# Output projection's second half in another block order with its sums shared with GpSimd, and the down projection's first splits moved ahead of the up projection's end

## The reference, cut to what matters

```python
h = h + merged @ w_out                                  # output projection, here called M
hn = rms_norm(h, mlp_norm_g)
h = h + jnp.square(jax.nn.relu(hn @ w_up)) @ w_down     # up projection U, down projection D
return h[:, N_META:]
```

## Time and profile before

| what | value |
|---|---|
| median of 3 runs | 1728.98 us (1727.06 to 1730.18) |
| profiled execution, its own time | 1731.9 us |
| its span | 1730.2 us |
| PE busy in the span | 1672.7 us, 97% |
| DVE, ACT, POOL busy | 923.8, 745.9, 384.5 us |
| M's second half | about 1035.5 to 1085 us |
| U | 1092.08 to about 1414 us |
| D | 1419.65 us to the end |

### The profile page before, as it was taken

One profiled execution on the slowest core, in us unless ns is written; L12 is line 12 of the kernel. 1 busy time (PEld: TensorE's weight loads), 2 busy tenths in 40 slices (PEclk: granted clock), 3 DMA queues, 4 the chain that ended last, 5 costly groups with the idle time before them and its releaser, 6 DMA issues.

```text
span 1730.2 us, 22462 instructions
## 1 busy us (share of the span) xinstructions
PE 1672.7 (97%) x7968; PEld 1385.3 (80%) x7968; DVE 923.8 (53%) x1712; ACT 745.9 (43%) x1528; POOL 384.5 (22%) x587
## 2 busy tenths in 40 slices
PE   7999999999999999898999999699999989999999
PEld 6777888878878888786888888488888878888887
DVE  4311256522355666645654425866666645766776
ACT  5322245423356666655212215555555444444443
POOL 1000001010037777675211001112211222200000
PEclk9999999999999999999999999899999999999999
DMA  6111113211123443426545223145444359843463
GB/s 193 50 49 48 46 60 116 71 61 49 49 67 76 99 97 70 101 56 173 185 144 188 74 61 123 48 148 175 147 140 154 138 196 345 280 127 98 123 194 98
DMA packets 109061, 204.08 MB, mean 118 GB/s; under 512 B 12560, under 2 KB 45376, under 8 KB 108960
## 3 DMA queue, kind: packets, MB, share of 16 engines
q1 hardware_dynamic: 71648, 104.88, 19.6%
q0 software_dynamic: 37312, 97.89, 17.9%
HBM read 139.55 MB, written 54.53 MB: 112 GB/s over the span
## 4 chain that ended last, share of the span: by engine, by line
PE 88%; DVE 6%; DMA 3%; ACT 2%; issue 1%; SPq 0%; POOL 0%; ACTq 0%; DVEq 0%
PE bank L701 27%; PE bank L706 26%; PE bank L705 26%; PE bank L916 2%; PE bank L952 1%; DMA RAW<-in_w_in 1%; PE bank L930 1%; DVE WL L1552 1%; DVE SOPL L1978 1%; PE bank L960 1%; PE bank L732 0%; PE bank L737 0%; PE bank L945 0%; PE bank L829 0%; PE bank L773 0%
## 5 line engine op out<-in xcount | busy, mean ns | idle before, releaser
L701 PE MATMUL bank<-WH,ADH 128*128 128x512 f32 x448 | 175.4, 392 | 5.6 <-DVE WL L2119 5.6
L701 PE MATMUL bank<-WH,HN 128*128 128x512 f32 x448 | 177.1, 395 | 3.3 <-DVE HN L1577 2.4
L1552 DVE TENSOR_TENSOR WL<-RAW,WH 128x512 fp32r<-128x512 f32 x152 | 100.0, 689 | 149.7 <-ACT WH L1137 149.0
L706 PE MATMUL bank<-WL,HN 128*128 128x512 f32 x448 | 175.4, 392 | 0.0
L705 PE MATMUL bank<-WH,HN 128*128 128x512 f32 x448 | 175.3, 391 | 0.0
L705 PE MATMUL bank<-WH,ADL 128*128 128x512 f32 x448 | 175.2, 391 | 0.0
L706 PE MATMUL bank<-WL,ADH 128*128 128x512 f32 x448 | 175.1, 391 | 0.0
L587 POOL TENSOR_SCALAR PR<-PR,RC 128x272 f32<-128x272 f32 x128 | 125.1, 1009 | 177.0 <-DVE RC L1866 176.5
L701 PE MATMUL bank<-HN,WH 128*128 128x512 f32 x384 | 153.5, 400 | 1.3 <-DVE WL L1552 1.3
L705 PE MATMUL bank<-HN,WL 128*128 128x512 f32 x384 | 151.4, 394 | 0.0
L706 PE MATMUL bank<-HN,WH 128*128 128x512 f32 x384 | 151.4, 394 | 0.0
(11 more groups left out here) (292 smaller groups left out, 3807.7 us busy)
## 6 DMA issues: line engine op xcount, KB each, us to landing
ARAW<-uop SPq DMA_DIRECT2D x112, 256.0 KB, 3.3
RAW<-in_w_in SPq DMA_DIRECT2D x104, 256.0 KB, 3.0
WRAW<-in_w_up SPq DMA_DIRECT2D x16, 1024.0 KB, 5.6
uop<-US POOLq DMA_DIRECT2D x64, 256.0 KB, 2.7
gates<-TB POOLq DMA_DIRECT2D x48, 256.0 KB, 2.4
uop<-UA POOLq DMA_DIRECT2D x48, 256.0 KB, 2.5
TH<-gates POOLq DMA_DIRECT2D x32, 256.0 KB, 3.0
RAWD<-in_w_down SPq DMA_DIRECT2D x32, 256.0 KB, 4.4
```

What stands on the lines that cost most here:

```text
L701: mm = pe.matmul(bank, ahi, bhi, start=first, stop=False, skip_group_check=onto)
L706: return pe.matmul(bank, ahi, blo, start=False, stop=last, skip_group_check=onto)
L1552: dve.tensor_tensor(WL[:, k, :], RAW[:, k % 4, :], WH[:, k, :].bitcast(F32), ALU.subtract)\
```

## The change

In M's second half the blocks go in the order `ORD` = 0 1 4 2 5 3 6 7 (place p, block b = ORD[p]); the first half keeps its order. Each hop is cut into `hop_first`, which on DVE goes ahead of `norm_h` and on ACT ahead of `square_h`, and a rest behind it; the last two subtractions of a heavy hop move to after the next eviction. The sum s2 goes from DVE to GpSimd beside s4. The four weight sums of U's group 0 go from DVE to GpSimd (`first_up_sums`). Six U weight tiles rather than four are split ahead of the last eviction. The last block gets its own `R22`/`S1B` tiles (over `ST`) and another order of its sums. The last transposes go into the middle of (0,1), behind its second k. At the seam between U and D the splits of D's steps 0 to 3 are done by ACT and DVE during U's last group (`EARLY`), and U's last sums `u_sums_a/b(15)` go behind step 4's split.

```diff
+EARLY = {3: (0,), 4: (1, 2), 5: (3,)}
+NEARLY = 4
+ORD = (0, 1, 4, 2, 5, 3, 6, 7)
...
+        R22, S1B = [at("R22", O_TB, [4, P]), at("R22L", O_ST, [4, P])], \
+            [at("S1B", O_TB + 2048, [4, P]), at("S1BL", O_ST + 2048, [4, P])]
...
+            def sums_s2_s4(b):                                   # GpSimd
+                pool.wait_ge(s3_rdy, b - 3)
+                pool.tensor_tensor(RA[:, 0, :, cols], sum_src(0, b), RA[:, 0, :, cols], ALU.subtract).then_inc(s2_rdy, 1)
                 pool.wait_ge(s2_rdy, b - 3)
                 pool.tensor_tensor(RA[:, 1, :, cols], RA[:, 1, :, cols], RA[:, 0, :, cols], ALU.add).then_inc(s4_rdy, 1)
+            def first_up_sums(later):        # GpSimd: XS2, XS3 if later, else XS0, XS1
...
+                pool.wait_ge(uraw[0], UR0 + 16)
+                pool.wait_ge(h1_st[0], HS0 + 64)
...
+            for p, b in enumerate(ORD):
+                if p == NB - 1:
+                    first_up_sums(False)
+                if p and ORD[p - 1] >= 4:
+                    sums_s2_s4(ORD[p - 1])
+                pool.wait_ge(xn_rdy, NB + 1 + p + 1)
                 pool.dma_start(h1s[b], H1[:, b, :]).then_inc(h1_st[b // 4], 16)
+            sums_s2_s4(NB - 1)
+            first_up_sums(True)
...
+                if f == 0 and t >= 2:                            # PE, up_product
+                    pe.wait_ge(hop_rdy, (17, 18, 18, 19, 20)[t - 2])
...
+                    if (f, t, k) == (0, 1, 1):
+                        transpose_h(NB - 1)
...
+            for p in range(NB):                                  # ACT
+                if p == NB - 1:
+                    for q in range(6):
                         up_hi(q)
+                if p >= 1:
+                    hop_hi_first(p - 1)
+                square_h(p)
+                if p >= 1:
+                    hop_hi(p - 1)
+            hop_hi_first(NB - 1)
             hop_hi(NB - 1)
+            for q in range(6, WS):
                 up_hi(q)
...
+                if f == UF - 1 and t in EARLY:                   # ACT and DVE, in U's loop
+                    for n in EARLY[t]:
+                        down_hi(0, n)
...
+            def hop_first(p):                                    # DVE
+                b, last = ORD[p], ORD[p] // (NB - 1)
                 if b < 4:
+                    dve.wait_ge(ra_hi, 2 * b + 1)
+                    lo_of(p, 0, A11).then_inc(a1_rdy, 1)
+                    return
...
+                dve.tensor_tensor(S1B[last][:, :, :], tile, R22[last][:, :, :], ALU.subtract).then_inc(s1_rdy, 1)
...
+                dve.tensor_tensor(R22[last][:, :, :], RA[:, 0, :, cols], tile, ALU.subtract).then_inc(s3_rdy, 1)
...
-                dve.tensor_tensor(RA[:, 0, :, cols], S1B[:, :, :], RA[:, 0, :, cols], ALU.subtract).then_inc(s2_rdy, 1)
...
+                            for q in range(6):                   # DVE, p == 7, ahead of the eviction
                                 up_lo(q)
...
                     if c == 1:
+                        if p >= 2 and ORD[p - 2] >= 4:
+                            lo_sums(ORD[p - 2], (2, 3))
+                        if p >= 1:
+                            hop_first(p - 1)
+                        norm_h(p)
+                        if p >= 1:
+                            hop_second(p - 1)
+            lo_sums(ORD[NB - 2], (2, 3))
+            hop_first(NB - 1)
+            lo_sums(NB - 1, range(4))
+            lo_a22(NB - 1)
+            for q in range(6, WS):
                 up_lo(q)
...
+                    if n >= NEARLY:                              # DVE, D's loop
+                        down_lo(t, k)
+                    if n == NEARLY:
+                        u_sums_a(UF - 1)
+                        u_sums_b(UF - 1)
```

More of the change, by code:

```diff
@@ L47 @@
 START = 1
+ORD = (0, 1, 4, 2, 5, 3, 6, 7)
+POS = {b: p for p, b in enumerate(ORD)}
 NPAIR = 8 * NB
@@ L1038, in _ @@
             for c in range(2):
-                for b in range(NB):
-                    j = DVE_F + 8 * c + b
+                for p in range(NB):
+                    b = p if c == 0 else ORD[p]
+                    j = DVE_F + 8 * c + p
                     pe.wait_ge(d_free, j - 1)
@@ L1418, in _, with hi_of @@
                     act.copy(MG[0][:, f, half * SL:(half + 1) * SL], TB[:, 1, :]).then_inc(e2_hi, 1)
[L1421 to L1424, removed]
+            def hi_of(p, u, dest):
+                b = ORD[p]
+                tile = B[2 + 2 * (p % 2) + u][:, :].rearrange("p (k t) -> p k t", k=4)
+                return act.copy(dest[:, 0, :, (b % 4) * P:(b % 4 + 1) * P], tile)
@@ L1425, in hop_hi, with raw_of, hop_hi_first @@
+            def raw_of(p, u):
+                tile = B[2 + 2 * (p % 2) + u][:, :].rearrange("p (k t) -> p k t", k=4)
+                return act.copy(RA[:, u, :, ORD[p] * P:(ORD[p] + 1) * P], tile)
+            def hop_hi_first(p):
+                b, last = ORD[p], ORD[p] // (NB - 1)
+                act.wait_ge(xt_full, 2 * (NB + 1) + 2 * p + 2)
                 if b < 4:
[L1426 to L1429, removed]
+                    hi_of(p, 0, A11)
+                    raw_of(p, 0).then_inc(ra_hi, 1)
@@ L1518, in _ @@
                     act.activation(UA12[:, :], R2T[:, :], ACT.Square).then_inc(u_sq, 1)
[L1520 to L1542, removed]
+            for n in range(NEARLY, 7 * UF):
+                down_hi(n // UF, n % UF)
         @block.vector
@@ new lines, in lo_a22, with lo_sums, hop_second @@
+            def lo_a22(p):
+                dve.wait_ge(h22_rdy, ORD[p] - 3)
+                lo_of(p, 1, A22).then_inc(hop_rdy, 1)
+            def lo_sums(b, places):
+                for n in places:
+                    i = sop_order(b)[n]
+                    dve.wait_ge(sop_hi, 4 * (b - 4) + n + 1)
+                    dve.tensor_tensor(sop_block(1, i, b), sum_src(i, b), sop_block(0, i, b).bitcast(F32),
+                                      ALU.subtract).then_inc(hop_rdy, 1)
+            def hop_second(p):
+                b = ORD[p]
+                if b < 4:
+                    dve.wait_ge(ra_hi, 2 * b + 2)
+                    lo_of(p, 1, A12).then_inc(a1_rdy, 1)
+                    dve.wait_ge(a1_rdy, 2 * b + 2)
@@ L1971, in hop_lo @@
[L1971 to L1973 removed]
+                lo_a22(p)
                 dve.wait_ge(hop_rdy, 5 * (b - 4) + 1)
                 dve.sem_inc(ht_free, 1)
[L1976 to L1979, removed]
+                lo_sums(b, (0, 1))
@@ L2070, in _ @@
                     up_lo(q + WS)
-            u_sums_a(UF - 1)
-            u_sums_b(UF - 1)
+                if f == UF - 1 and t in EARLY:
+                    for n in EARLY[t]:
+                        down_lo(0, n)
             def down_sum(t, k):
```

177 lines of the change are left out of this document (98 added, 79 removed).

## The result

The changed kernel takes 1717.43 us (median of 4 runs, 1713.92 to 1720.08) against 1728.02 us (4 runs) of the kernel before on the same chip: ratio 0.9937, 95% interval 0.9915 to 0.9958, that is 10.9 us less, with 7.3 and 14.7 as the interval's ends. Timed again beside three other kernels it gave 0.9921 (0.9908 to 0.9935), 13.7 us less. The forecast of 14.7 us less lies at the edge of the first interval and inside the second; 1717.43 is in the range.

What follows compares the result with a forecast made beforehand. PE bounds the kernel, busy 1672.7 of 1730.2 us, so only its losses can be won. Handover 6.5 plus seam 8.2 make 14.7 us off the median 1728.98: 1714.3, range 1708.8 to 1721.3.

Steps and rivals of the forecast that it cites:

- The seam: Between U and D: 5.75 us of PE idle and 2.49 us of low clock go, 8.2 us in sum.
- DVE keeps up until M's end: M's second half: DVE's places cost 5.2 and 4.4 us, below PE's 6.37 per block, until M's matmuls end.
- Meetings: M's second half: GpSimd sums and DVE instructions with two SBUF inputs exclude each other, 0 to 1.28 us per meeting.
- if these sums are stretched past 2 us: Stated sign of being wrong, for the sums on GpSimd in M's second half.
- turns or DVE first: End of M: with mutual delay (0,4) starts at 1117.6; if DVE always wins, at 1117.0; 6.5 us gain taken.
- WRAW1's load: M's place 7: U's second weight load lands at 1087.5 (1086.4 without meetings), a new wait for ACT and DVE.
- the low clock behind this wait is as before: Behind the wait before (0,4): idle of 2 to 3 us in both kernels, so no change in low clock.
- the stretch ahead of T0: From the start to PE's first transposes in M's second half; no change was counted there.
- handover: From M to U: (0,4) starts earlier, at 1117.6 instead of 1123.85; gain taken as 6.5 us.
- sums cost DVE nothing: Rival, M's second half: GpSimd sums cost DVE only waiting for results; 19.6 us gain, time 1709.4, chance 0.17.
- GpSimd is the new end of M: Rival, M's end: (0,4) starts where it did, only the seam's 8.2 us are left; 1720.8, chance 0.14.
- The norm never missed its place: Stated sign of being wrong: the norm misses its place in M's earlier blocks.

Runs made afterwards that it cites:

- seam_only: The kernel before with only the U/D seam change (early splits, moved last U sums); ratio to before 0.9955, 7.8 us less.
- order_only: The changed kernel with the old seam of U and D (no early splits, U's last sums back ahead of D's loop); ratio to before 0.9966, 5.9 us less.
- last_on_dve: wraw1_early with block 7's s2 and s4 and weight sums XS2 and XS3 on DVE, the other sums staying on GpSimd; ratio to before 0.9901.
- store_first: wraw1_early with GpSimd waiting for the norm and issuing the block's store before making s2 and s4; ratio to before 0.9928.
- early_mix_r2t: Changed kernel with earlier second weight load, R2T's copy before the eleventh cast, block 7's and weight sums on DVE; blocks 4 to 6 shared; 1708.58 us, ratio 0.9876.
- wraw1_early: The changed kernel with U's second weight load waiting only for the stores of blocks 0 and 1; ratio to before 0.9911.
- after_again: The changed kernel unaltered, traced and timed a second time on the same chip; ratio to before 0.9921.
- s2_on_dve: The changed kernel with each heavy hop's s2 back on DVE behind s3, GpSimd keeping s4 and the four weight sums; ratio to before 0.9904.
- all_dve: The changed kernel with every sum on DVE and none on GpSimd; ratio to before 0.9904.

## Why the prediction was right

*The seam* (5.75 + 2.49 = 8.2): D's first matmul follows U's last, the window from 1411 has a clock of 1.00 and PE busy throughout. `seam_only` measured 7.8 us, and in `order_only` the wait of 5.58 us is back. The moved sums and stores cost nothing, as said; the changed kernel even waits twice for an activation tile in U's last group (0.87 and 0.63 us of ACT) without PE noticing.

*DVE keeps up until M's end*: yes, the first wait of PE is behind M. I had said that the wait of 5.36 before (0,0) would be gone; 0.76 us of it are left: `up_lo(0)` starts at 1086.48, behind the light hop.

*Meetings*: right in kind and in both directions. The norm was stretched by 1.02 in places 3 and 5 and by 0.73 at place 7, s4 by 0.85. By the letter of my text this was a sign of being wrong ("if these sums are stretched past 2 us"): s4 took 2.13 to 2.14 us in three hops of four. But the count itself has s4 wait for the whole norm (1.28 us and its own 1.28, about 2.5), and its end in place 5 came 0.25 us before the forecast (1078.95 on the axis of before, against 1079.2). The threshold did not fit the sum; the sum held. The exclusion that the Trainium skill states on the page "SBUF — State Buffer", section "Who interferes with whom", holds in this trace for the direction that no row of before showed: a GpSimd sum of 1.29 us took 2.14 behind a norm. Of my two counts for the end, turns or DVE first, it was turns.

*WRAW1's load*: wait and place right, 1 us too early. On the axis of before (1.82 less) the cast behind it starts at 1088.5, not 1087.5; store to load took 3.80 us and not 2.96, load to cast 5.8 and not 5.3. The last eviction 1091.6 (forecast 1090.9), the norm's end 1096.0 (1095.5), (0,2) 1107.5 (1107.6), the sum into R1T 1110.3 (1110.7), (0,4) 1117.2 (1117.6). That the end fits so well is luck in part: the norm ended 0.5 us late, and from there to (0,2) it took 11.5 us where I had counted 12.1. In the two other traces of this code up to (0,4) the gain was 7.35 and 7.56 us and not 6.64.

*What was mis-sized*: "the low clock behind this wait is as before". It cost 1.0 to 1.3 us more in three traces of this code, and 1.6 less in `seam_only`'s, than in before's. And I took the stretch ahead of T0 as fixed, where two traces of one program differ by 4.6 us. These two, +1.30 and +1.82, are what lies between forecast and profiled execution: handover 6.64, idle of the seam 5.75, low clock behind it 2.53, together 14.92 against my 14.7; less 1.30 and 1.82 that is 11.80, the difference of the two spans. In the other two traces of this code the larger gain up to (0,4) and the loss behind it nearly cancel (7.35 less 1.04 and 7.56 less 1.29, about 6.3 us, against my 6.5). I had foreseen neither, so the sum is nearer than its terms by luck.

*The rivals*: "sums cost DVE nothing" is refuted by the stretched rows, and its price of 4.9 us was not what was to be had: taking all sums off GpSimd brings 1.4 to 2.3. "GpSimd is the new end of M" was half true. Its late sums are in the chain (s2 of block 7, 1102.70; `last_on_dve`, which takes them off, brings 2.07 us), but did not eat the gain. The norm never missed its place.

## What to carry to other kernels

When an engine that is behind does not sit idle in the same places as its neighbour, first spread its work over the places where it idles and move copies that others wait for ahead of work that itself waits; here order, early splits, an earlier load and one moved copy gave 21 us, with no sum on GpSimd. Hand elementwise work to GpSimd where DVE does not run with two SBUF inputs at that time: a sum of 0.7 us that went over cost DVE up to 1.1 us per meeting in the changed kernel and 1.5 in `store_first`. At the end of the chain that was a loss of 2 us; in blocks 4 to 6 it was neither a loss nor a gain that could be told (`early_mix_r2t`). And when the order of blocks changes, look at every transfer that waits for "the first four".

## What the runs showed of the hardware that I had not expected

Turns under load: at the end of the chain, with both engines having work ready, GpSimd's sums and DVE's subtractions alternated, one each, at 1.7 us a pair (rows 1105.16 to 1108.03 and 1105.81 to 1107.52 above; `wraw1_early` and `store_first` show the same there). A DVE instruction with an input in PSUM went through beside them at 0.68 us (the A22 subtraction at 1079.55, while s4 ran).

The clock behind PE's idle was not a function of that idle alone. The mean granted clock over the 7 us from (0,4) on was 1.00 behind an idle of 1.42 us (`seam_only`) and 1.46 (`store_first`), and 0.76 behind 2.08 (before). Behind 3.16 to 3.18 us it was 0.56, 0.59 and 0.56 in the changed kernel, `after_again` and `order_only`, but 0.76 in `s2_on_dve`, `wraw1_early` and `all_dve`. What decides between these two is not shown.
